# Experts ranked by token count on the chip, full ones in pairs of 64 slots, the emptiest four at a time in 32 slots, with weight loads addressed by registers

## Chip, core and metric

The kernel runs on 1 core of one Trainium2 chip. The metric is the device time of one execution in microseconds (us). A difference under about 0.2% (some 4.6 us) can't be told from no change.

## The reference, cut to the part that the change touches

The whole model is one hybrid layer (attention, retention, mixture of experts) and then two more layers with feed-forward blocks. The change touches only the routed experts of the first layer. There are 256 tokens of 1024 features and 64 experts; each token goes to 8 of them.

```python
def moe_ffn(h, router_w, router_bias, w1, w3, w2, sw1, sw3, sw2):
    scores = sigmoid(h @ router_w)                  # 256 x 64
    ...                                             # 4 of 8 groups, then top_e: 8 experts a token
    wts = wts / sum(wts) * ROUTED_SCALE
    for each expert e, for the tokens tok sent to e, with weight wt:
        xb = h[tok]
        yb = (silu(xb @ w1[e]) * (xb @ w3[e])) @ w2[e]     # 1024 -> 256 -> 1024, float32
        acc[tok] += yb * wt
    shared = (silu(h @ sw1) * (h @ sw3)) @ sw2
    return acc + shared
```

One expert's w1 and w3 are 2 MB together and its w2 is 1 MB, so the 64 experts have 192 MB of weights. How many tokens an expert gets is known only after the router has run. Evaluating the router on the inputs gives, for experts 0 to 7: 39, 36, 18, 42, 68, 25, 120 and 42 tokens. Four experts have more than 64 tokens (120, 77, 68, 67). The 64 counts add up to 2048. With experts 0 to 3 kept in front and the other 60 sorted, rank 4 has 120 tokens, rank 8 has 60, rank 39 has 25, rank 40 has 23 and rank 63 has 5.

## The kernel before

**Steps.** The routed experts are computed in 48 steps (`N_PAIRS`). A step fills the 128 partitions with 128 token slots. 32 of the steps are base steps: experts 2q and 2q+1 with 64 slots each. 16 are overflow steps: two blocks of 64 slots each for tokens that don't fit into an expert's first 64. Which expert an overflow block belongs to is decided on the chip. The order is written out by hand in `pair_order`: `"bbbb" + "obb" * 12 + "ob" * 4`. An overflow step runs on TensorE whether or not it has tokens.

**TensorE.** Each iteration i runs `gate_up(i)`, `hidden_turn(i - 1)` (two transposes), `gather_in(i + 1)` (eight transposes of the gathered token rows) and `down(i - 1)`. `gate_up` has 16 matmuls of a 128x64 stationary tile of tokens against 128x512 weights; the two experts of a step use different halves of the array's columns. `down` has 8 such matmuls. In the first 11 iterations `table(k)` runs too: small matmuls with one-hot matrices `OH` that turn the router's result into a token index and weight for each slot (`TAB`, then `IDX` and `WS` by VectorE's `post(k)`).

**Base weights.** SyncE (SP) issues 96 loads of 2 MB, two "up" and one "down" a base step, in the order of `NEED`, into five cells of the buffer `ring` (printed `ring<-in_exp_up`, `ring<-in_exp_down`). Load n waits until the load CELLS = 5 places before it has been used (`cell_read`) and until load n - 2 has landed (`cell_in`), so two are in flight.

**Gathers, overflow weights and scatters.** GpSimd (POOL) issues all indirect DMAs, in order. In turn i it issues the gather of the token rows for step i + 4 (L2041), then possibly the overflow weights (`overflow(k, "up")` and `overflow(k, "down")`, L2059, two DMAs each), then the scatter of step i - 1's result rows to `moe_rows` (L2068). Rows with an index outside the bounds are skipped, so an empty overflow block moves no weights; TensorE still waits for its semaphores `over_up` and `over_down`. The up weights of overflow step k are issued in the turn after the overflow step before it, and the down weights one turn later.

**Start.** SP loads five cells, then stores the normalised tokens to `h2_rows` (L744) as soon as their transposes are copied. The gathers wait for that store and for `posted`.

**After the steps.** SP fetches the first six weight tiles of the next feed-forward block and then reads `moe_rows` back in 8 loads.

Of the kernel before, what the change touches and what calls it, by code (L numbers as in the profile page):

```python
# [45 lines left out]
CAP = 64  # L46
N_BASE = N_EXP // 2
N_OVER = 16
N_PAIRS = N_BASE + N_OVER
N_BLOCKS = 2 * N_OVER  # L50
CELLS = 5
# [9 lines left out]
def pair_order():  # L61

    base, over = iter(range(N_BASE)), iter(range(N_BASE, N_PAIRS))
    kinds = "bbbb" + "obb" * 12 + "ob" * 4
    return [next(base) if k == "b" else next(over) for k in kinds]

def chunk_order():

    out = [0, 1]  # L70
    base, over = list(range(2, N_BASE // 2)), list(range(N_BASE // 2, N_PAIRS // 2))
    while base or over:
        out += over[:1] + base[:2]
        over, base = over[1:], base[2:]
    return out
# [3 lines left out]
PAIRS = pair_order()  # L79
CHUNKS = chunk_order()  # L80
# [13 lines left out]
def shape_constants():  # L94
# [49 lines left out]
    for h in range(4):  # L144
# [4 lines left out]
    own = np.stack([8 * p, 8 * (P + p), p + 1, P + p + 1], axis=1).astype(np.float32)  # L149
    rows = np.zeros((P, P), np.float32)  # L150
    rows[0:N_EXP] = p[0:N_EXP, None] * P + p[None, :] + 1
    moe = np.concatenate([wide(np.arange(1, CAP + 1)), own, wide(CAP * np.arange(N_BLOCKS)), wide(np.arange(N_BLOCKS)),
                          rows], axis=1).astype(np.float32)
    return {"k_before": before, "k_moe": moe, "k_heads": heads, "k_always": always, "k_dist": dist, "k_dirs": dirs, "k_chunk": chunk, "k_rot": rot}

def build(nc, A, out, h2_rows, moe_rows):
# [6 lines left out]
    with ctx:  # L164
# [34 lines left out]
        MC = sb("moe_const", [P, 260])  # L199
        IDX = sb("moe_index", [P, N_PAIRS, 2], I32)  # L200
        EIDX = sb("moe_expert_rows", [P, N_BLOCKS], I32)
        WS = sb("moe_slot_weight", [P, N_PAIRS])
# [120 lines left out]
        plan("sh_gate", 2, free=("hidden_ready", 1))  # L323
        plan("sh_up", 0, free=("hidden_ready", 1))
        plan("rank", 1)
        for n in range(4):
            plan(f"sh_y{n}", 3 + n, full=("units_down", 1))
        plan("ov_a", 0)
        plan("ov_b", 1)
        plan("ov_p", 7, free=("posted", 3))  # L330
        plan("moe_tab", 7, full=("table_full", len(CHUNKS)), free=("posted", len(CHUNKS)))
        for i in range(N_PAIRS):
            plan(f"mx{i}a", 0)
            plan(f"mx{i}b", 1)
            plan(f"mg{i}", 2 + i % 2)
            plan(f"mh{i}", 4)
            plan(f"my{i}a", 5)
            plan(f"my{i}b", 6)
# [3 lines left out]
        BASE_AT = [i for i in range(N_PAIRS) if PAIRS[i] < N_BASE]  # L342
        OVER_AT = [i for i in range(N_PAIRS) if PAIRS[i] >= N_BASE]
        NEED = []
        for i in range(N_PAIRS + 1):
            if i in BASE_AT:
                NEED += [(BASE_AT.index(i), "up_a"), (BASE_AT.index(i), "up_b")]
            if i - 1 in BASE_AT:
                NEED.append((BASE_AT.index(i - 1), "down"))
        CELL = {part: n for n, part in enumerate(NEED)}  # L350

        def cell(q, part):

            b = 7 + 2 * ((CELL[q, part] + 1) % CELLS)
            return BIG[:, b:b + 2, :]

        def cell_read(n):

            q, part = NEED[n]
            return uses[f"my{BASE_AT[q]}b" if part == "down" else f"mg{BASE_AT[q]}"].full  # L360

        def cell_in(n):

            return (f"cell_in{n % CELLS}", 16 * (n // CELLS + 1))
# [4 lines left out]

        posts_needed = {lp: CHUNKS.index(lp // 2) + 1 for lp in range(N_PAIRS)}  # L370
# [193 lines left out]
        OVER_DOWN = [BIG[:, 5 + e, :] for e in range(2)]  # L564
# [4 lines left out]
        P1 = MEAN[:, 0:4 * N_PAIRS].rearrange("p (l t b) -> p l t b", t=2, b=2)  # L569
        DW = K0[:, 256:256 + 12 * N_PAIRS].rearrange("p (l t b c) -> p l t b c", t=2, b=2, c=3)  # L570
# [3 lines left out]
        C_SLOT, C_ROW0, C_TOK, C_J64, C_J = MC[:, 0:64], MC[:, 64:66], MC[:, 66:68], MC[:, 68:100], MC[:, 100:132]  # L574
        C_EROW = MC[0:N_EXP, 132:260]
        OV_T = MIX[0:N_EXP, 4:7, :]
        OV_LO, OV_HI, OV_SEL, OV_TMP = (MIX[0:N_EXP, 7, a:a + n] for a, n in ((0, 1), (1, 1), (32, 32), (64, 32)))
        TAB = PS[:, 7, 0:6 * N_PAIRS].rearrange("p (l c) -> p l c", c=6)
        OVP = PS[:, 7, 288:480].rearrange("p (q t j) -> p q t j", q=3, t=2)
        OVE = PS[:, 7, 480:512]  # L580
# [66 lines left out]
        OV_N, OV_END, OV_BEG = (AXS[:, 6, 64 * a:64 * a + 64] for a in range(3))  # L647
        OV_OFF = AXS[:, 6, 192:256]
# [9 lines left out]
        CHKF = sb("chunk_row", [P, T])  # L658

# [26 lines left out]
        MASKED, RANKED, CHOSEN, ADDED = 1, 2, 3, 4  # L686
# [6 lines left out]
        def _(sp):  # L693
# [24 lines left out]
            def base(q, part, *free):  # L718

                n = CELL[q, part]  # L720
# [6 lines left out]
                if part == "down":  # L727
                    src = A["exp_down"][2 * q * P:(2 * q + 2) * P, :].rearrange("(e p) n -> p e n", e=2)
                else:
                    expert = 2 * q + (part == "up_b")  # L730
                    src = A["exp_up"][expert * P:(expert + 1) * P, :].rearrange("p (a n) -> p a n", a=2)
                sp.dma_start(cell(q, part), src).then_inc(S(cell_in(n)[0]), 16)
# [12 lines left out]
            for q, part in NEED[CELLS:]:  # L745
                base(q, part)
# [32 lines left out]
        def _(pe):  # L779
# [365 lines left out]
            for i in range(N_PAIRS):  # L1145
# [3 lines left out]
                if i + 1 < N_PAIRS:  # L1149
                    gather_in(i + 1)  # L1150
# [2036 lines left out]
```

## Time and profile before

| what | value |
|---|---|
| three runs | 2315.76, 2318.59, 2319.61 us; median 2318.59 us |
| profiled execution, its span | 2327.8 us |
| TensorE matmul busy | 2174.5 us, 93% |
| VectorE, ScalarE, GpSimd busy | 57%, 14%, 9% |
| HBM read / written | 634.49 / 27.26 MB |

The profile gives no time of its own for the profiled execution beside the span from its first to its last instruction; the span is 9.2 us above the median of the runs, which were executed without the profiler. Busy shares are averages over stages with different limits. Times in the rows below are counted from the start of the span. In lists by line, `x32` counts instructions; one float32 matmul of the program appears as two records.

### The profile page before, as it was taken

To read this page: it belongs to the slowest core of one execution; us is meant where nothing else is said; L and a number is where in the kernel's file an instruction comes from. 1 tells how busy PE (TensorE), PEld (TensorE's weight loads), DVE (VectorE), ACT (ScalarE), POOL (GpSimd) and SP (SyncE) were. 2 spreads that over 40 slices of the span, in tenths; PEclk is the share of its full clock that TensorE was granted. 3 is DMA by queue.
4 is the path that set the end of the run, shared out by engine and by line. 5 is a ranking of instruction groups with operands and counts; after the bars stand their busy time and mean duration, and the time that the engine had idled before them with its cause. 6 is when DMAs were issued, how large, how long until landed. Compare 5 with 4: busy or idle time off the path is not lost.

```text
span 2327.8 us, 32193 instructions
## 1 busy us (share of the span) xinstructions
PE 2174.5 (93%) x13280; PEld 1635.1 (70%) x13280; DVE 1329.9 (57%) x2488; ACT 322.2 (14%) x614; POOL 214.1 (9%) x264
## 2 busy tenths in 40 slices
PE   6999898989999989699999989999999998989997
PEld 3577753433333333499988868899989986579996
DVE  4567432321111111388875766798888876557774
ACT  2133100101111111100001341000000001430000
POOL 0000021223222222000000000000000000000000
PEclk9999899999999999899999999999999998999999
DMA  9865449989999986656666400566856663223441
GB/s 369 307 245 212 169 188 417 404 337 386 388 386 383 376 327 249 243 198 223 240 228 239 146 32 1 199 237 217 292 199 250 210 248 120 73 73 133 175 153 48
DMA packets 85969, 542.28 MB, mean 233 GB/s; under 512 B 24540, under 2 KB 24796, under 8 KB 33472
## 3 DMA queue, kind: packets, MB, share of 16 engines
q1 hardware_dynamic: 48448, 413.49, 46.5%
q0 software_dynamic: 36656, 124.83, 14.6%
q8 instruction: 106, 1.74, 0.3%
q10 hardware_dynamic: 720, 1.91, 0.2%
q14 instruction: 39, 0.32, 0.0%
HBM read 634.49 MB, written 27.26 MB: 284 GB/s over the span
## 4 chain that ended last, share of the span: by engine, by line
PE 84%; DVE 7%; DMA 7%; issue 1%; ACT 1%; POOL 0%; SPq 0%; DVEq 0%; POOLq 0%
PE ps L1190 30%; PE ps L1111 13%; PE ps L1140 6%; PE ps L979 3%; PE ps L1340 3%; PE ps L1245 3%; DMA ring<-in_exp_up,moe_expert_rows 3%; PE ps L1208 3%; PE ps L842 3%; PE ps L1090 2%; PE ps L868 1%; PE ps L1319 1%; DVE ring L2143 1%; PE ps L1586 1%; DVE x_streams L2143 1%
## 5 line engine op out<-in xcount | busy, mean ns | idle before, releaser
L1190 PEld LDWEIGHTS ps<-h,ring 128*128 128x128 f32 x4480 | 500.9, 192 | 0.2
L1190 PE MATMUL ps<-h,ring 128*128 128x128 f32 x4480 | 500.9, 275 | 0.0
L2143 DVE TENSOR_TENSOR ring<-ring 128x512 f32<-128x512 f32 (+5 forms) x411 | 349.3, 868 | 37.1 <-DMA ring<-moe_rows 22.6
L1111 PE MATMUL ps<-ring,h 128*64 128x512 f32 x1536 | 348.1, 607 | 22.9 <-DMA ring<-in_exp_up,moe_expert_rows 16.3
L1111 PEld LDWEIGHTS ps<-ring,h 128*64 128x64 f32 x1536 | 112.7, 140 | 242.7 <-issue 242.5
L2227 DVE SCALAR_TENSOR_TENSOR ring<-ring,ada_acc 128x1024 f32<-128x1024 f32 x152 | 179.6, 1222 | 42.0 <-DMA ring<-in_mod_w 30.3
L2537 DVE COPY hidden<-ps 128x256 f32<-128x256 f32 x48 | 20.4, 424 | 317.5 <-PE ps L1121 317.5
L1140 PE MATMUL ps<-ring,hidden 128*64 128x512 f32 x768 | 177.1, 603 | 7.2 <-DMA ring<-in_exp_down 4.4
L1190 PE MATMUL ps<-ring 128*128 128x128 f32 x1464 | 166.7, 275 | 0.0
L1190 PEld LDWEIGHTS ps<-ring 128*128 128x128 f32 x1464 | 165.4, 192 | 0.2
L2020 POOL DMA_DIRECT2D ring<-in_mod_w x72 | 38.7, 538 | 1000.9 <-DVE ring L2227 728.9
L1140 PEld LDWEIGHTS ps<-ring,hidden 128*64 128x64 f32 x768 | 52.2, 137 | 98.0 <-issue 98.0
L1811 ACT ACTIVATE silu_gate<-hidden 128x512 f32<-128x512 f32 x40 | 25.2, 631 | 492.0 <-DVE hidden L2143 492.0
L979 PE MATMUL ps<-h,ring 128*128 128x256 f32 x384 | 87.9, 390 | 3.2 <-DVE small L2362 1.1
L979 PEld LDWEIGHTS ps<-h,ring 128*128 128x128 f32 x384 | 74.5, 196 | 15.9 <-DVE small L2362 1.5
L1208 PE MATMUL ps<-h,ring 128*128 128x256 f32 x256 | 66.5, 428 | 19.5 <-DVE h L2148 19.5
L1340 PE MATMUL ps<-h,ring 128*128 128x256 f32 x384 | 84.1, 380 | 0.0
L1340 PEld LDWEIGHTS ps<-h,ring 128*128 128x128 f32 x384 | 72.7, 190 | 10.1 <-issue 0.3
L1779 ACT ACTIVATE silu_gate<-ps 128x256 f32<-128x256 f32 x48 | 18.4, 383 | 436.6 <-PE ps L1111 436.6
L2633 DVE COPY mean<-ps 128x256 f32<-128x256 f32 (+1 forms) x52 | 20.5, 393 | 101.5 <-PE ps L1190 101.4
L1208 PEld LDWEIGHTS ps<-h,ring 128*128 128x128 f32 x256 | 55.6, 219 | 30.5 <-issue 21.0
L1245 PE MATMUL ps<-ring 128*128 128x256 f32 x352 | 76.6, 379 | 0.0
(443 smaller groups left out, 2598.6 us busy)
## 6 DMA issues: line engine op xcount, KB each, us to landing
ring<-in_exp_up SPq DMA_DIRECT2D x64, 2048.0 KB, 10.8
ring<-in_mod_w POOLq DMA_DIRECT2D x72, 1024.0 KB, 6.8
ring<-in_exp_down SPq DMA_DIRECT2D x32, 2048.0 KB, 10.1
ring<-in_ffn_gate SPq DMA_DIRECT2D x44, 1024.0 KB, 4.8
ring<-in_ffn_up SPq DMA_DIRECT2D x44, 1024.0 KB, 6.2
ring<-in_ffn_down SPq DMA_DIRECT2D x32, 1024.0 KB, 4.9
ring<-in_ada_late POOLq DMA_DIRECT2D x16, 1024.0 KB, 5.2
ring<-in_hyb_in SPq DMA_DIRECT2D x16, 1024.0 KB, 6.0
```

The source lines that it names most:

```text
L842: last = mm(b[:, 0:(2 * T if wide else T)], w[:, kt, :], H[:, :, kt, :] if wide else H[:, 1, kt, :], start=kt == 0, stop=kt == KT - 1)
L979: last = mm(b[:, m * T:(m + 1) * T], w[:, kt, m * P:(m + 1) * P], MIX[:, kt, :], start=kt == 0 and m == 0, stop=kt == KT - 1 and m == 1)
L1090: last = nc.tensor.transpose(bs[k // 4][:, (k % 4) * P:(k % 4 + 1) * P], XG[i % LOOKAHEAD][:, k * P:(k + 1) * P], IDN)
L1111: last = mm(b[64 * e:64 * e + 64, :], xt[:, k // 2, k % 2, 64 * e:64 * e + 64], ws[e][:, k, :], start=k == 0, stop=k == KT - 1)
L1140: last = mm(bs[y][64 * e:64 * e + 64, :], ht[:, m, 64 * e:64 * e + 64], w[e][:, m, y * 512:(y + 1) * 512], start=m == 0, stop=m == 1)
L1190: ins = mm(dst, a[:, kt, :], b[:, kt, :], start=first and n < 2 and kt == 0, stop=last and n > 4 and kt == half - 1)
L1208: ins = mm(PS[:, u.bank, m * T:(m + 1) * T], w[:, kt, m * P:(m + 1) * P], U_IN[:, kt, :], start=kt == 0 and m == 0, stop=kt == KT - 1 and ...
L1245: ins = mm(y_of(6 + m), w[:, kt, m * P:(m + 1) * P], HIDA[:, k0 + kt, :], start=c == 0 and kt == 0 and m == 0, stop=z and kt == DOWN_KT[c] ...
L1340: last = mm(b[:, m * T:(m + 1) * T], w[:, kt, m * P:(m + 1) * P], U_IN[:, kt, :], start=kt == 0, stop=kt == KT - 1)
L2020: pool.dma_start(MR[:, slot, :], src).then_inc(S(f"mod_in{slot}"), 16)
L2143: return V.tensor_tensor(out_, a, b, op)
L2227: ins = V.scalar_tensor_tensor(out=w[:, h], in0=w[:, h], scalar=1.0, in1=row, op0=M, op1=M, accum_out=dst)
```

## The change

The experts are ranked on the chip by token count (counts are compared pairwise with VectorE, experts 0 to 3 are kept as ranks 0 to 3). 42 steps replace the 48, in a new fixed order. `pair` steps hold two experts of 64 slots. `second` steps hold the slots 64 to 127 of the pair just before (ranks 4 to 7), with the same weights. `quad` steps hold four experts of 32 slots (ranks 40 to 63). `over` steps, now 14, hold two overflow blocks. The numbers of `pair`, `quad`, `second` and `over` steps are 20, 6, 2 and 14. SP reads the expert's number from SBUF into a register for all loads but those of ranks 0 to 3. There are six cells. Overflow down weights now use the same buffer as the up weights.

```diff
-CAP = 64
-N_OVER = 16
-CELLS = 5
+CAP = 32
+FIXED = 4
+N_OVER = 14
+CELLS = 6
...
+def step_order():
+    kinds = "ff" + "dso" * 2 + "pqoppo" * 4 + "pqopo" + "qopop"
...
+def cap_of(rank):
+    if rank >= min(r for kind, r in STEPS if kind == "quad"):
+        return CAP
+    return 4 * CAP if ("second", rank - rank % 2) in STEPS else 2 * CAP
...
-        OVER_DOWN = [BIG[:, 5 + e, :] for e in range(2)]
+        OVER_DOWN = [BIG[:, 1 + 2 * e, :] for e in range(2)]
...
 # SP
+                if rank < FIXED:
+                    up = A["exp_up"][rank].rearrange("p (a n) -> p a n", a=2)
+                    downs = [A["exp_down"][rank + e] for e in range(2)]
                 else:
+                    sp.wait_ge(S("posted"), 1)
+                    who = [sp.value_load(EXI[0:1, rank + e:rank + e + 1], min_val=0, max_val=N_EXP - 1)
+                           for e in range(1 if part == "up" else 2)]
+                    up = A["exp_up"][bass.ds(who[0], 1)].rearrange("e p (a n) -> p (e a) n", a=2)
+                    downs = [A["exp_down"][bass.ds(w, 1)].rearrange("e p n -> p (e n)") for w in who]
+                if part == "up":
+                    sp.dma_start(cell(at, part, x), up).then_inc(landed, 16)
+                else:
+                    for e in range(2):
+                        sp.dma_start(cell(at, part, x)[:, e, :], downs[e]).then_inc(landed, 16)
...
             shared("shared_down", BIG[:, 4, :], (2,))
-            base(0, "down", released[23])
+            base(4, released[23])
+            base(5, released[21], released[22])
             for n in range(4):
                 wait(sp, uses[f"h2t{n}"].free)
             for tt in range(TT):
                 sp.dma_start(h2_rows[tt * P:(tt + 1) * P, :], H2T[:, tt, :]).then_inc(S("h2_stored"), 16)
...
-                last = uses[f"mg{o}"].full if slot < 3 else uses[f"my{o}b"].full if slot < 5 else cell_read(
-                    max(n for n in range(len(NEED)) if n % CELLS == 4))
+                last = uses[f"my{o}b"].full if slot < 3 else cell_read(
+                    max(n for n in range(len(NEED)) if n % CELLS == (5 if slot < 5 else 4)))
...
 # PE
+            def table(k):
+                pe.wait_ge(S("onehot"), k + 1)
+                for a in range(2):
+                    i = 2 * k + a
+                    dw = DW_F[:, i] if i < 2 else DW_S[:, i - 2]
+                    for tt in range(TT):
+                        for g in range(4):
+                            last = mm(TAB[32 * g:32 * g + 32, i, :], OH[k % 2][:, 8 * a + 4 * tt + g, :], dw[:, tt, g, :],
+                                      start=tt == 0, stop=tt == 1)
+                last.then_inc(S("table_full"), 1)
...
+                z = P // len(ws)
                 for k in range(KT):
-                    for e in range(2):
-                        last = mm(b[64 * e:64 * e + 64, :], xt[:, k // 2, k % 2, 64 * e:64 * e + 64], ws[e][:, k, :],
+                    for e, w in enumerate(ws):
+                        last = mm(b[z * e:z * e + z, :], xt[:, k // 2, k % 2, z * e:z * e + z], w[:, k, :],
                                   start=k == 0, stop=k == KT - 1)
...
 # POOL
             def overflow(k, kind):
-                if k == 0:
-                    pool.wait_ge(S("posted"), 3)
-                    if kind == "up":
-                        pool.wait_ge(S("units_down"), 1)
-                    else:
-                        for slot in (3, 4):
-                            wait(pool, released[18 + slot])
+                if kind == "down":
+                    wait(pool, uses[f"mg{OVER_AT[k]}"].full)
+                elif k == 0:
+                    pool.wait_ge(S("posted"), 2)
+                    pool.wait_ge(S("units_down"), 1)
                 else:
-                    o = OVER_AT[k - 1]
-                    wait(pool, uses[f"mg{o}" if kind == "up" else f"my{o}b"].full)
+                    wait(pool, uses[f"my{OVER_AT[k - 1]}b"].full)
...
-            for k in range(1, N_OVER):
-                up_turn[OVER_AT[k - 1] + 1] = k
-                down_turn[OVER_AT[k - 1] + 2] = k
+            up_turn = {OVER_AT[k - 1] + 2 if k else 0: k for k in range(N_OVER)}
...
-                if i in down_turn:
-                    overflow(down_turn[i], "down")
+                if i - 1 in OVER_AT:
+                    overflow(OVER_AT.index(i - 1), "down")
```

The tables of two steps now take 16 matmuls of a 128x32 stationary tile and 2 columns (4 of 128x128 and 6 columns before), and there are 21 of them (24 before). Ranking adds a chain of small operations on VectorE, TensorE and ScalarE between the router and the first gather.

**Where the order changes, first place: POOL near the end of the steps.** Each row is an indirect DMA: L2059 (L2161 in the changed kernel) loads overflow weights, L2041 (L2146) gathers rows for a later step, L2068 (L2170) scatters a result. Before:

```order
L2059 DMA ring<-in_exp_up,moe_expert_rows 128x4096 x2
L2068 DMA moe_rows<-ring,moe_index 2048x1024
L2041 DMA h<-h_rows,moe_index 128x1024
L2059 DMA ring<-in_exp_down,moe_expert_rows 128x2048 x2
L2068 DMA moe_rows<-ring,moe_index 2048x1024
```

The same engine in the middle of the changed kernel's steps, where overflow steps are three apart:

```order
L2146 DMA x_streams<-h_rows,moe_index 128x1024
L2161 DMA ring<-in_exp_down,moe_expert_rows 128x2048 x2
L2170 DMA moe_rows<-squares,moe_index 2048x1024
L2146 DMA x_streams<-h_rows,moe_index 128x1024
L2161 DMA ring<-in_exp_up,moe_expert_rows 128x4096 x2
L2170 DMA moe_rows<-ring,moe_index 2048x1024
```

The down load of an overflow step now comes first, one turn after that step's own gate_up, and the next overflow step's up load follows one turn later. Before, the up load came first and both were issued ahead of the step that uses them.

**Second place: SP between the prologue's loads and the first steps.** L744 (L803) is the store of the token rows; TENSOR_LOAD and ISA rows are the register reads. Before:

```order
L716 DMA ring<-in_shared_down 128x2048
L732 DMA ring<-in_exp_down 128x2x2048
L744 DMA h_rows<-squares 128x1024 x2
L732 DMA ring<-in_exp_up 128x4096 x2
L732 DMA ring<-in_exp_down 128x2x2048
```

And in the changed kernel:

```order
L764 DMA ring<-in_shared_down 128x2048
L790 DMA ring<-in_exp_down 128x2048 x2
L782 TENSOR_LOAD chunk_row
L782 ISA x2
L787 ISA
L787 DMA ring<-in_exp_up 128x4096
L803 DMA h_rows<-squares 128x1024 x2
```

The store of the token rows now stands behind a load that needs the ranking.

## Rows read from the trace of the kernel before

**Rows 1.** Windows of the step stage: engine busy times, granted clock, DMA share, GB/s.

```profile
316.00:499.00 183.00, 164.39 (x828) 74.16 (x828) 54.25 (x196) 16.75 (x32) 36.12 (x36) 0.93 0.91 372
499.00:841.00 342.00, 342.00 (x1690) 130.74 (x1689) 63.88 (x117) 46.12 (x88) 96.41 (x96) 1.00 0.98 383
841.00:944.00 103.00, 91.89 (x438) 34.46 (x436) 17.61 (x33) 12.23 (x23) 23.10 (x23) 0.95 0.64 244
```

**Rows 2.** Chain of waits, one step in the middle: start, duration, what.

```profile
504.19 6.87 PE ps L1111 x32
...
512.37 3.58 PE ps L1140 x16
515.95 6.87 PE ps L1111 x32
```

**Rows 3.** Chain of waits over the whole step stage, first, stalled and last pieces.

```profile
315.99 9.09 PE ps L1111 x32
...
326.11 1.68 PE ps L1059 x16
...
400.34 25.27 DMA ring<-in_exp_up,moe_expert_rows
...
850.77 14.96 DMA ring<-in_exp_up,moe_expert_rows
...
939.72 3.67 PE ps L1140 x16
...
953.01 19.81 DMA ring<-moe_rows
```

**Rows 4.** DMA by queue in 500 to 850 us: packets, MB, share.

```profile
q1 hardware_dynamic: 11132, 124.98, 89.9%
q0 software_dynamic: 13966, 8.89, 8.0%
```

**Rows 5.** Queue q0 alone, 300 to 325 us, then 325 to 500 us.

```profile
q0 software_dynamic: 576, 1.35, 18.1%
...
q0 software_dynamic: 5042, 17.62, 25.0%
```

**Rows 6.** Timeline at 857 us: a result copied, then POOL's issues.

```profile
857.04 0.69 DVE L2546 COPY ring<-ps 128x512 f32<-128x512 f32 x1 [2.90 <-PE ps L1140]
858.60 1.02 POOL L2068 DMA_INDIRECT moe_rows<-ring,moe_index  x1 [6.84 <-DVE ring L2546]
859.92 1.01 POOL L2041 DMA_INDIRECT h<-h_rows,moe_index  x1 [0.31 <-issue]
...
862.53 0.99 POOL L2059 DMA_INDIRECT ring<-in_exp_down,moe_expert_rows  x1 [0.30 <-issue]
```

**Rows 7.** L2059 (overflow loads), 500 to 850 us, then 840 to 855 us.

```profile
DMA to landing us min/median/max: 3.6/4.8/21.3
...
  PE ps L1111: 8.9, 1
...
DMA to landing us min/median/max: 4.7/9.8/15.0
```

**Rows 8.** Groups by line and shape: busy us, mean ns, idle before.

```profile
L842 PE MATMUL ps<-h,ring 128*128 128x512 f32 x96 | 42.2, 592 | 0.0
L1111 PE MATMUL ps<-ring,h 128*64 128x512 f32 x1536 | 348.1, 607 | 22.9 <-DMA ring<-in_exp_up,moe_expert_rows 16.3 <-DMA ring<-in_exp_up 5.6 <-issue 1.0
L1111 PEld LDWEIGHTS ps<-ring,h 128*64 128x64 f32 x1536 | 112.7, 140 | 242.7 <-issue 242.5
L813 PEld LDWEIGHTS ps<-ring,silu_c 128*2 128x2 f32 x128 | 5.7, 85 | 10.4 <-ACT hidden L1658 2.2 <-issue 0.8
```

**Rows 9.** Timeline of the start: SP's store, ScalarE, first gather.

```profile
285.02 0.83 SPq L744 DMA_DIRECT2D h_rows<-squares  x2
...
290.15 0.60 ACT L1760 ACTIVATE silu_gate<-ps 128x512 f32<-128x512 f32 x1 [3.91 <-PE ps L1031]
...
308.58 1.07 POOL L2041 DMA_INDIRECT x_streams<-h_rows,moe_index  x1 [75.82 <-DVE moe_index L2151]
```

More of the change, by code:

```diff
@@ L58, with step_blocks @@
 SILU_AT = {10: (0,), 11: (1,), 12: (2, 3), 13: (4, 5)}
[L61 to L75, printed above, removed]
+def step_order():
+    kinds = "ff" + "dso" * 2 + "pqoppo" * 4 + "pqopo" + "qopop"
+    pair, quad, over = 0, 2 * sum(kinds.count(k) for k in "fdp"), 0
+    steps = []
+    for k in kinds:
+        if k == "s":
+            steps.append(("second", pair - 2))
+        elif k == "o":
+            steps.append(("over", over))
+            over += 1
+        elif k == "q":
+            steps.append(("quad", quad))
+            quad += 4
+        else:
+            steps.append(("pair", pair))
+            pair += 2
+    return steps
+STEPS = step_order()
+N_STEPS = len(STEPS)
+N_TABLES = N_STEPS // 2
+SORTED = 4 * (N_STEPS - 2)
+def cap_of(rank):
+    if rank >= min(r for kind, r in STEPS if kind == "quad"):
+        return CAP
+    return 4 * CAP if ("second", rank - rank % 2) in STEPS else 2 * CAP
+def step_blocks(step):
+    kind, r = step
+    if kind == "quad":
+        return [(r + g, 0) for g in range(4)]
+    base = 2 * CAP if kind == "second" else 0
+    return [(r + g // 2, base + CAP * (g % 2)) for g in range(4)]
 HYB_COLS = [0, 256, 512, 768, 1536, 1792, 1024, 1280, 2120, 2376, 2632, 2888, 3144, 3400, 3664, 3920]
-PAIRS = pair_order()
-CHUNKS = chunk_order()
 PARAMS = {}
@@ L323, in build @@
         plan("sh_gate", 2, free=("hidden_ready", 1))
+        plan("rank", 1)
+        plan("ov_d", 7)
         plan("sh_up", 0, free=("hidden_ready", 1))
-        plan("rank", 1)
+        plan("ov_p", 1)
+        plan("ov_c", 7)
         for n in range(4):
             plan(f"sh_y{n}", 3 + n, full=("units_down", 1))
[L328 to L332, printed above, removed]
+        plan("sel_p", 0)
+        plan("sel_d", 2)
+        plan("sel_w", 1)
+        plan("moe_tab", 7, full=("table_full", N_TABLES), free=("posted", N_TABLES))
+        for i in range(N_STEPS):
             plan(f"mx{i}a", 0)
@@ L1085, in gather_in @@
+            for kt in range(4, KT):
+                last = shared_down(kt)
+            last.then_inc(S("units_down"), 1)
+            for name in ("sel_d", "sel_w"):
+                wait(pe, uses[name].free)
+            pe.wait_ge(S("posted"), 1)
+            table(1)
             def gather_in(i):
@@ L1102, in gate_up @@
                 else:
-                    parts = [(BASE_AT.index(i), "up_a"), (BASE_AT.index(i), "up_b")]
+                    at = i - 1 if kind == "second" else i
+                    parts = [(at, "up", x) for x in range(4 if kind == "quad" else 2)]
                     for part in parts:
@@ L1131, in down @@
                 else:
-                    part = (BASE_AT.index(i), "down")
-                    wait(pe, cell_in(CELL[part]))
-                    ws = [cell(*part)[:, e, :] for e in range(2)]
+                    at = i - 1 if kind == "second" else i
+                    parts = [(at, "down", x) for x in range(2 if kind == "quad" else 1)]
+                    for part in parts:
+                        wait(pe, cell_in(CELL[part]))
+                    ws = [cell(*part)[:, e, :] for part in parts for e in range(2)]
                 w = [x.rearrange("p (m n) -> p m n", m=2) for x in ws]
+                z = P // len(w)
                 ht = HID[:, i % 2, 1, :].rearrange("p (m n) -> p m n", m=2)
@@ L1144, in _ @@
             gather_in(0)
-            for i in range(N_PAIRS):
+            for i in range(N_STEPS):
                 gate_up(i)
```

393 lines of the change are left out of this document (215 added, 178 removed).

## The prediction

> **What bounds the kernel now.** I read three views in this order: the windows of the step stage, the chain of waits there, and the DMA queues. In the windows the reader is to see two resources that are full at once. From 499 to 841 us TensorE is busy all 342 us and the DMA share is 0.98 [rows 1]. The chain tells which of the two decides: it runs through TensorE alone, one step every 515.95 - 504.19 = 11.76 us, of which gate_up is 6.87 and down 3.58 [rows 2]. So this stretch is bound by TensorE, with DMA just behind it. The first stretch, 316 to 499 us, holds 12 steps. They should take 141.1 us, the tables of 11 steps add 11 x 1.7 to 2.0 = 19 to 22, and the first gate_up, at the lower clock after an idle time, 2.2 (9.09 against 6.87) [rows 2, 3]. That makes about 164; the rest, 19 us, is waiting, and the long piece in it is the 25.27 us load of overflow weights [rows 3]. These are real: queue q0 moved 17.62 MB from 325 to 500 us [rows 5], and four blocks of 3.15 MB are 12.6 of them. The number of blocks is four by the counts of the inputs (68, 120, 77, 67 tokens against 64 slots). That the trace ran these inputs shows in the first four gathers: 1.35 MB [rows 5] are 330 rows of 4096 bytes, and experts 0 to 7 are fetched by 330 of their tokens (39, 36, 18, 42, 64, 25, 64, 42). The last stretch has one stall: an overflow load that moves nothing took 15.0 us to land, and TensorE waited 8.9 us for it [rows 3, 7]. Steps end at 939.72 + 3.67 = 943.4 us.
>
> **What the change removes.** 48 steps become 42, which is 6 x 11.76 = 70.6 us of TensorE. After ranking, no expert has more tokens than its slots (rank 4 has 120 of 128, rank 8 has 60 of 64, rank 40 has 23 of 32), so the four real blocks and their 12.6 MB go. All 14 overflow steps are then empty. TensorE runs them all the same.
>
> **What DMA needs.** A load costs the queues 0.899 x 350 us / (124.98 / 2.097) = 5.28 us in the middle of the stage, and a gathered or scattered row 0.08 x 350 us / 2170 (8.89 MB / 4096 bytes) = 12.9 ns, skipped rows included [rows 4]. Where less else runs a load can be a little cheaper; I take 5.1. The 96 loads and 2 x 2048 rows are about 543 us, more than the 42 x 11.76 = 494 us of TensorE. So DMA may become the bound, and the 70.6 us can't all be won.
>
> **The start.** Half of the shared up-projection ends before ScalarE's silu at 290.15 [rows 9]. Ranking, four transposes and the other half follow, by the spacing of the old program to about 298; the first table and two small matmuls 2, VectorE's posting 2: posted at 302. Then SP reads a register, issues a 2 MB load and only then the store of the rows, which before was issued at 285.02 [rows 9]. The store lands behind that load: 5.1 + 4 + 1 makes 312. The gather takes 1.07 to issue [rows 9], some 4 to land, transposes and copy 3: first gate_up at 321, 5 us later than 315.99 [rows 3]. Bounds: -4 if the store overtakes the load, +9 if the ranking chain is slower.
>
> **Tables.** Each now has 32 records. The group nearest to a record with 32 stationary columns is the weight load of 2 columns, 5.7 us / 128 = 45 ns, below, and that of 64 columns, 112.7 / 1536 = 73 ns, above [rows 8]. I take 55: 1.76 us a table.
>
> **Quad steps.** 64 records in gate_up instead of 32. A record of 512 columns on the undivided array takes 42.2 / 96 = 440 ns, one on half the columns 348.1 / 1536 = 227 [rows 8]: two halves run side by side at 1.94 times. If four quarters do too, a record must start each 110 ns, more than the 73 ns that a 64-column weight load needs, so 6.87 us stays. I take that; the other bound is two at a time, 10.45 us more a quad step. The Trainium skill, TensorE: Matmul & The Clock Gate, in the table of tiled matmuls, gives 3.07 times for four tiles instead of 4. By it a quad step would be 3.2 us longer and six of them 19 us, mostly hidden by DMA; the rows speak for less loss, since two tiles lose only 3%. The sum keeps the rows' value.
>
> **A new wait.** An overflow step's down weights used to be issued ahead of the step, now only after the next gather. Let T be the end of the down-projection before. POOL's second DMA starts at T + 5.5 (857.04 to 862.53) [rows 6]; TensorE wants it after one gate_up and ten transposes, at T + 8.2. With a landing of 4.8, the median [rows 7], the stall is 2.1 us. Up weights start at T + 5.5 too, T now being the end of the last overflow step's down. If overflow steps are three apart TensorE wants them at T + 11.8: no stall. The last three (steps 36, 38, 40) are two apart: 5.5 + 4.8 = 10.3 us each, and 2.2 each for the lower clock after such an idle time. While TensorE stands, SP's loads behind its cells stand too.
>
> **The sum.** Steps 0 to 7: 8 x 11.76 + 2.2 + 16 tables x 1.76 = 124.5, ending at 445.5; TensorE bounds here, since eight steps need only 12 loads. Steps 8 to 31: TensorE needs 24 x 11.76 + 5.3 (tables) + 8 x 2.1 = 304; DMA needs 60 loads less 6 already in the cells, 54 x 5.1 = 275, and 2610 rows, 34, over a share of 0.98: 315. DMA decides, ending at 760.5. Steps 32 to 41: 117.6 + 4 x 2.1 + 3 x 12.5 = 163.5, ending at 924. One late landing as at 850 us: 9. Steps end at 933 instead of 943.4: -10. Behind them, three of the six feed-forward tiles are fetched only after the last step and come ahead of the read of `moe_rows` that takes 19.81 us [rows 3]: +3. Net -7 us: span 2321 instead of 2327.8. The span is 9.2 above the median of the runs, so the prediction is 2318.6 - 7 = 2312 us.
>
> SP's register reads (one for an up, two for a down load) aren't in the trace. I cost them at nothing, because load n waits for load n - 2 and load n - 1 still has its 5 us to go. If a read and issue take more than 5 us, each microsecond above costs up to 90 us in all; nothing suggests it.
>
> **Rivals.**
> - *Late landings (slower).* Landings between 500 and 850 us reach 21.3 us, and one of 15.0 stopped TensorE for 8.9 [rows 7]. Before, most such landings had some 12 us or more to spare; now 28 pairs stand on the path. One landing of 15 costs 12 us on a down and 9 on an up load. Beyond the one in my sum, the gain is gone with the second. One in five late makes 5 to 6: +35 to +45, about 2350. For it speaks that the DMA share will be near 1 in steps 8 to 31; against it that a late one is partly covered where TensorE waits for weights anyway, and that the median is 4.8. 
> - *Cheap extras (faster).* Tables at 45 ns a record (-6), store overtaking (-4), no late landing (-9), loads and steps interleaving well (-8): 2285.
> - *Quarters at half speed (slower).* 62.7 us of TensorE, of which some 20 to 25 hide under DMA: +40, 2350.
> - *The change does little*: what six steps save goes to loads and extras to within 4.6 us, 2318.
>
> **How the numbers follow.** My forecast -7 has a chance of 0.36 (its own range 2298 to 2326), cheap extras 0.21, late landings 0.27, quarters or register reads 0.10, nothing 0.06. The range over these is 2282 to 2356. Faster by over 0.2% (4.6 us): 0.24 of the forecast's case and 0.21 give 0.45. Within 0.2%: 0.08 and 0.05 give 0.13. Slower: 0.42.
>
> **What would show it.** First gate_up near 321 us; 42 steps; no q0 transfer of overflow weights; quad gate_ups of 6.9 us (13.7 if two at a time); waits of 2 us before each overflow down and of 10 us before the last three overflow gate_ups; loads the releaser in steps 8 to 31. Wrong if POOL's overflow landings, not loads, end most waits of TensorE in the middle stretch, or if quad steps are long.

## The result, and the profile after

The changed kernel takes **2386.79 us** (median of 4 runs, 2381.97 to 2393.83) against 2319.1 (2315.76 to 2322.53) for the kernel before, run beside it: ratio 1.0288, interval 1.0257 to 1.0319. That is 68 us slower, where I had forecast 2312 and a range up to 2356. The profiled execution has a span of 2380.2 us, 52 above the 2327.8 of before; the other 15 us come from how the two profiled spans stand to these medians (6.6 below, 8.7 above), which no row explains. Ratios and intervals leave out executions in which the chip was in its slower state, of which there was one, in run 9.

Line numbers after: L1183 `gather_in`, L1207 `gate_up`, L1240 `down`, L1129 `table`, L2161 `overflow`. First the windows of the changed kernel, cut as in [rows 1] (columns as there).

```profile
316.00:499.00 183.00, 162.50 (x1372) 68.17 (x1374) 48.65 (x142) 18.93 (x36) 41.81 (x41) 0.92 0.77 299
499.00:841.00 342.00, 285.70 (x1516) 107.72 (x1514) 50.49 (x92) 36.28 (x69) 76.91 (x77) 0.93 0.92 364
841.00:944.00 103.00, 60.02 (x308) 22.25 (x304) 9.95 (x19) 7.29 (x14) 14.11 (x15) 0.80 0.62 241
```

In the middle stretch TensorE was busy all 342 us before and is now for 285.7, and DMA fell from 0.98 to 0.92. **Neither resource is full any more**, so something is waiting that is neither TensorE's work nor the bytes. The waits of TensorE from 310 to 1010 us name it (total us, times, longest):

```profile
PE ps L1240 <- DMA ring<-in_exp_down,moe_expert_rows: 77.3, 13, 16.8
PE ps L1207 <- DMA ring<-in_exp_up,moe_expert_rows: 29.7, 3, 15.4
PE ps L1207 <- DMA ring<-in_exp_up: 22.2, 5, 6.0
PE ps L1183 <- DMA x_streams<-h_rows,moe_index: 7.0, 1, 7.0
```

107 us are waits for overflow transfers that move nothing. Before, waits for overflow transfers came to 17.5 us in four times; two of them, of 6.3 and 8.9 us, were for transfers that moved nothing. The 7.0 us of L1183 lie ahead of the first gate_up. The chain of waits in the middle shows the pattern, where [rows 2] had TensorE alone (start, duration, what):

```profile
563.53 17.40 DMA ring<-in_exp_down,moe_expert_rows
581.07 6.54 PE ps L1240 x16
...
616.65 7.94 DMA ring<-in_exp_down,moe_expert_rows
624.73 5.20 PE ps L1240 x16
...
717.82 3.65 PE ps L1240 x16
721.47 7.00 PE ps L1207 x64
```

One overflow step of each two lands after some 17 us, the other after 5 to 8. After ten of the 13 waits for downs the same 16 records of `down` take 5.2 to 6.6 us; after the other three (1.2, 2.4 and 2.9 us long) they take 3.65. The granted clock over the records at 581.07 is 0.51, the lower of its two levels:

```profile
581.00:587.00 6.00, 5.93 (x15) 1.91 (x16) 0.00 (x0) 0.60 (x1) 0.00 (x0) 0.51 0.99 406
```

Over the two later stretches it is 0.93 and 0.80 where it was 1.00 and 0.95.

Last, the start and the end of the chain:

```profile
302.29 10.46 DMA h_rows<-squares
...
320.73 8.74 PE ps L1207 x32
...
989.30 3.67 PE ps L1240 x16
...
994.55 8.35 DMA moe_rows<-ring,moe_index
...
1006.85 22.12 DMA ring<-moe_rows
```

The first gate_up starts at 320.73 and the steps end at 989.30 + 3.67 = 993.0, 49.6 later than before; from there to the end of the `moe_rows` reads (1028.97) it is 36.0 us, against 29.4 before. Together that is 56 us; the rest of the program took 3.8 us less than before, which makes the 52 of the spans.

The waits themselves, in the timeline of TensorE (start, duration, line, shape, count, idle time before and its releaser):

```profile
546.05 7.04 PE L1207 MATMUL ps<-ring,h 128*64 128x512 f32 x32
...
561.96 8.78 PE L1207 MATMUL ps<-ring,h 128*64 128x512 f32 x32 [3.99 <-DMA ring<-in_exp_up]
...
581.07 6.54 PE L1240 MATMUL ps<-ring,hidden 128*64 128x512 f32 x16 [9.02 <-DMA ring<-in_exp_down,moe_expert_rows]
...
595.72 3.65 PE L1240 MATMUL ps<-ring,hidden 128*64 128x512 f32 x16
...
862.92 5.57 PE L1240 MATMUL ps<-ring,hidden 128*64 128x512 f32 x16 [16.80 <-DMA ring<-in_exp_down,moe_expert_rows]
```

The 13 waits for downs are 7.2, 9.0, 8.7, 7.3 and 16.8 us behind the five landings of 17 to 23 us, together 49, and eight of 1.2 to 6.5, together 28. Each of the five is preceded by one of the five waits for a base up load (561.96 here): there the loads are behind already.

**Where TensorE's 672.3 us between the first gate_up and the end of the steps go.** 42 steps of 11.76 are 493.9. A step with the tables of two steps takes 12.61 (its gate_up starts at 344.06 and the next at 356.67), 0.85 more; nine of these and one with a single table are 8. The waits are 77.3 + 29.7 + 22.2 and 1.9 of other kinds, 131. The lower clock shows in the busy time of the groups. By line and shape outside quad steps (columns as in [rows 8]):

```profile
L1207 PE MATMUL ps<-ring,h 128*64 128x512 f32 x1152 | 268.7, 621 | 53.2 <-DMA ring<-in_exp_up,moe_expert_rows 29.7 <-DMA ring<-in_exp_up 22.2 <-issue 1.3
L1240 PE MATMUL ps<-ring,hidden 128*64 128x512 f32 x576 | 153.1, 680 | 78.9 <-DMA ring<-in_exp_down,moe_expert_rows 77.3 <-DVE hidden L2641 1.6
```

These are 36 `gate_up` of 32 records and 36 `down` of 16. At the full clock they take 7.04 and 3.65 us (546.05 and 595.72 above), so 36 x 7.04 = 253.4 and 36 x 3.65 = 131.4. `gate_up` is 15 us above that and `down` 22, together 37. All terms add up to 670 of the 672.3.

### The profile page after: what moved, and what is told of

Its sections match the earlier page's. It is cut to its first block, busy times and chain, and to the rows that moved or that the text cites. A ratio compares the mean times of both kernels' runs of the same rounds, so it can differ in the third digit from the quotient of the medians.

```text
span 2380.2 us, 33491 instructions
## 1 busy us (share of the span) xinstructions
PE 2111.9 (89%) x13714; PEld 1600.9 (67%) x13714; DVE 1308.8 (55%) x2409; ACT 313.6 (13%) x599; POOL 196.3 (8%) x244
## 3 DMA queue, kind: packets, MB, share of 16 engines
q0 software_dynamic: 33776, 112.24, 13.1%
## 4 chain that ended last, share of the span: by engine, by line
PE 78%; DMA 10%; DVE 7%; issue 2%; POOL 2%; ACT 1%; SPq 0%; POOLq 0%; DVEq 0%
PE ps L1290 30%; PE ps L1207 9%; PE ps L1240 7%; DMA ring<-in_exp_down,moe_expert_rows 6%; PE ps L1038 3%; PE ps L1440 3%; PE ps L1345 3%; PE ps L901 3%; PE ps L1308 3%; PE ps L927 1%; PE ps L1419 1%; PE ps L1183 1%; DVE ring L2241 1%; PE ps L1686 1%; DMA ring<-moe_rows 1%
## 5 line engine op out<-in xcount | busy, mean ns | idle before, releaser
L1207 PE MATMUL ps<-ring,h 128*64 128x512 f32 (+1 forms) x1536 | 311.1, 614 | 53.3 <-DMA ring<-in_exp_up,moe_expert_rows 29.7
L1207 PEld LDWEIGHTS ps<-ring,h 128*64 128x64 f32 (+1 forms) x1536 | 104.2, 135 | 248.8 <-issue 248.3
L1240 PE MATMUL ps<-ring,hidden 128*64 128x512 f32 (+1 forms) x768 | 174.9, 659 | 78.9 <-DMA ring<-in_exp_down,moe_expert_rows 77.3
L1240 PEld LDWEIGHTS ps<-ring,hidden 128*64 128x64 f32 (+1 forms) x768 | 51.7, 144 | 172.2 <-issue 172.2
L1440 PEld LDWEIGHTS ps<-h,ring 128*128 128x128 f32 x384 | 72.7, 190 | 10.1 <-issue 0.3
L2650 DVE COPY squares<-ps 128x512 f32<-128x512 f32 x20 | 13.8, 691 | 117.5 <-PE ps L1240 117.5
## 6 DMA issues: line engine op xcount, KB each, us to landing
ring<-in_exp_up SPq DMA_DIRECT2D x64, 2048.0 KB, 10.1
```

What stands on the lines that cost most here:

```text
L1207: last = mm(b[z * e:z * e + z, :], xt[:, k // 2, k % 2, z * e:z * e + z], w[:, k, :], start=k == 0, stop=k == KT - 1)
L1240: last = mm(bs[y][z * e:z * e + z, :], ht[:, m, z * e:z * e + z], w[e][:, m, y * 512:(y + 1) * 512], start=m == 0, stop=m == 1)
L1440: last = mm(b[:, m * T:(m + 1) * T], w[:, kt, m * P:(m + 1) * P], U_IN[:, kt, :], start=kt == 0, stop=kt == KT - 1)
```

## Experiments

All are timed against the kernel before. The first four undo or isolate one thing each.

**1. Down transfers issued one turn sooner.** POOL issues them in the overflow step's own turn, as soon as its gate_up is done and ahead of the scatter.

```diff
-                if i - 1 in OVER_AT:
-                    overflow(OVER_AT.index(i - 1), "down")
+                if i in OVER_AT:
+                    overflow(OVER_AT.index(i), "down")
```

> One edit to the changed kernel: POOL issues an overflow step's down weights in that step's own turn, ahead of the scatter of the step before, instead of one turn later behind that scatter and a gather. Theory 'late landings': TensorE's waits for overflow down weights (77.3 us in 13 waits in the changed kernel's profile) fall under 10 us, since the issue comes some 8 us earlier against 5.9 us of mean wait and the 17 us landings still cost a little; waits for base weights grow by 10 to 30 us because DMA catches up as the bound. Total 2317 to 2340 us instead of 2387. Rival 'DMA throughput is the bound': the waits only change their name to base weights and the total stays at 2377 or more.

Measured: **2347.89 us** (ratio 1.011, 1.0075 to 1.0146), 39 less than the changed kernel. Waits of TensorE:

```profile
PE ps L1207 <- DMA ring<-in_exp_up,moe_expert_rows: 72.0, 7, 16.2
...
PE ps L1240 <- DMA ring<-in_exp_down,moe_expert_rows: 1.6, 1, 1.6
```

The waits for downs go from 77.3 to 1.6 us. Those for overflow ups rise from 29.7 to 72.0, where I had expected base weights to take over (these stay at 23), and the time stands a little above the range that I gave.

**2. No overflow transfers.** The 14 overflow steps still run on TensorE, with whatever lies in their buffers; their DMAs and waits are left out.

> Leaves out all indirect loads of overflow weights and TensorE's waits for them; the 14 overflow steps still run, on whatever the buffer holds (their slots are empty). Theory 'late landings': this is the ceiling of what those loads cost, 77.3 + 29.7 us of waits less what the base weights then take over: 2285 to 2315 us. Rival 'DMA throughput': 2370 or more, with the waits on base weights.

Measured: **2290.42 us** (ratio 0.9868, 0.9845 to 0.9892). Of TensorE's waits for weights in the steps this one group stays:

```profile
PE ps L1206 <- DMA ring<-in_exp_up: 57.4, 10, 9.4
```

The change without its overflow transfers is 29 us faster than before. The 28 pairs of empty transfers cost 96 us.

**3. Smaller packets.** Each 2 MB up load as two of 1 MB, 8 KB a packet instead of 16.

```diff
-                    sp.dma_start(cell(at, part, x), up).then_inc(landed, 16)
+                    for h in range(2):
+                        sp.dma_start(cell(at, part, x)[:, h, :], up[:, h, :]).then_inc(landed, 16)
```

> Each 2 MB up load of the base weights is issued as two DMAs of 1 MB, whose packets are 8 KB instead of 16 KB; the bytes are the same. Theory 'skipped rows take turns with the packets of the weight loads': the landings of 17 to 23 us of the overflow down loads behind quad steps fall to about 10 us or less, and the total by 20 to 40 us (2347 to 2367). If the packets' size has nothing to do with it, the landings and the total stay (2380 to 2394).

Measured: **2388.62 us** (1.0289, 1.0263 to 1.0316): no change. The longest landing fell from 22.7 to 14.4 us and the waits for downs from 77.3 to 50.0, but the ups became late in seven places:

```profile
PE ps L1208 <- DMA ring<-in_exp_up,moe_expert_rows: 56.8, 7, 15.1
PE ps L1241 <- DMA ring<-in_exp_down,moe_expert_rows: 50.0, 13, 6.8
```

Packets of half the size go with a shorter longest landing, though not with the 10 us or less that I had expected; the sum of the two waits (107) did not move. What was won on one was lost on the other.

**4. No registers.** Loads take their expert from a fixed address (the weights are then not those of the ranks), so SP reads no register.

> All base weight loads take fixed addresses (the expert's number is the rank), so SP reads no registers; the experts' weights are then not those of the ranks, the work and bytes are the same. My prediction costs register reads at nothing: total within 6 us of the changed kernel's 2387. Rival 'register reads delay the loads': 10 us or more faster.

Measured: **2379.39 us** (1.0263, 1.0235 to 1.0291), 7 less, with an interval that overlaps that of the changed kernel. In the profiled executions the start is 3.6 us sooner, since no load waits for the ranking any more: the store goes out at 285.26 instead of 301.91, and the first gate_up starts at 317.10. But the steps end at 992.7, against 993.0 in the changed kernel: the waits for base ups fall from 22.2 to 14.5, those for overflow downs rise from 77.3 to 86.1. So the reads are not the slowdown, and this run can't tell their cost from nothing.

**5. Both transfers sooner.** As run 1, and the up transfers too one turn sooner (`OVER_AT[k - 1] + 1`).

> As the run with the early down load, and also the next overflow step's up weights one turn earlier, ahead of the scatter of the overflow step's result: issued about 4 us sooner after the buffer is free (T + 1.6 instead of T + 5.5). Theory 'late landings': waits for overflow up weights fall from 72 us to 30 us or less, and the total to 2300 to 2325 us, between the 2348 of the early down load and the 2290 of no overflow loads. Rival: the landing takes longer the earlier it is issued, since the same packets are in front; then 2335 or more.

Measured: **2322.25 us** (1.0015, 0.9996 to 1.0034): 65 less than the changed kernel, and no different from before. What is left of the waits:

```profile
PE ps L1207 <- DMA ring<-in_exp_up,moe_expert_rows: 37.4, 7, 15.8
PE ps L1207 <- DMA ring<-in_exp_up: 23.4, 6, 4.6
...
PE ps L1240 <- DMA ring<-in_exp_down,moe_expert_rows: 16.5, 5, 6.4
```

**6. And the row store ahead of the register load.** As run 5, with SP storing `h2_rows` before it asks for the sixth cell.

> As before, and SP stores the token rows ahead of the first register-addressed load. My prediction's start term (5 us later than before) says that this gives about 5 us or a bit more: first gate_up at 311 to 316 us instead of 320.7, total 4 to 9 us under that of both early issues.

Measured: **2317.93 us** (0.9984, 0.9969 to 0.9999), 4 less than run 5. The store goes out at 285.45 and the first gate_up starts at 317.28, against 320.10 in run 5: 3 us sooner, less than the 311 to 316 that I had expected. The load in front of the store costs some 4 us of the 10.46 that the store takes to land.

**7. Five cells, the overflow downs in a buffer of their own,** both overflow transfers issued where the kernel before issues them; ranking, 42 steps and registers stay, the store goes first.

```diff
-CELLS = 6
-OVER_DOWN = [BIG[:, 1 + 2 * e, :] for e in range(2)]
+CELLS = 5
+OVER_DOWN = [BIG[:, 5 + e, :] for e in range(2)]
```

> Undoes the buffer part of the change and keeps the ranking, the 42 steps and the register addresses: five cells, overflow down weights in a buffer of their own, both overflow loads issued at the turns of the kernel before, the token rows stored before any register-addressed load, the feed-forward tiles fetched as before. Theory 'late landings': TensorE's waits for overflow weights are under 20 us and the total comes near the run without overflow loads: 2285 to 2305 us, faster than the kernel before. Rival 'one cell less starves the quad steps', which need four cells at once: 2320 or more with the waits on base weights.

Measured: **2322.98 us** (1.0028, 1.0011 to 1.0045). The overflow waits are gone but for 5.6 us, and base weights take their place (the downs another 13.2 us):

```profile
PE ps L1206 <- DMA ring<-in_exp_up: 65.3, 11, 9.1
...
PE ps L1206 <- DMA ring<-in_exp_up,moe_expert_rows: 5.6, 2, 3.4
```

The rival in the expectation was right: with one cell less the loads run out. The sixth cell was paid for with the overflow downs' buffer. With the late issue that trade loses some 60 us against this run; with both transfers early (run 6) it gains 5.

**8. Quads one step earlier** in the pattern (`"qpoppo"` for `"pqoppo"`), since each late landing followed a quad step.

> Only the order of steps: each quad step stands before the pair step instead of after it, so that an overflow step never follows a quad step except in the last group. In the changed kernel the down weights of overflow steps right behind a quad land 17 to 23 us after issue, the others 5 to 8. Theory 'packets of up loads in front': a quad frees four cells at once and SP fills them with 16 KB packets just when POOL issues; with a pair between, the landings of 17 us fall to 5 to 8 us, total 2340 to 2370. If the delay belongs to every second overflow step whatever its neighbour, the total stays at 2380 or more.

Measured: **2396.76 us** (1.032, 1.0292 to 1.0348). Every second overflow step is still late, now with two pairs ahead of it where the quad was:

```profile
622.39 6.73 DMA ring<-in_exp_down,moe_expert_rows
...
671.04 14.01 DMA ring<-in_exp_down,moe_expert_rows
```

So the quad neighbour was not the reason, and my first theory here fell. What the late ones of the changed kernel share shows in SP's and POOL's timeline (start, duration until the last of the group, line, what):

```profile
550.63 12.31 SPq L787 DMA_DIRECT2D ring<-in_exp_up  x3
563.53 0.99 POOL L2161 DMA_INDIRECT ring<-in_exp_down,moe_expert_rows  x1 [0.30 <-issue]
...
604.71 7.51 SPq L787 DMA_DIRECT2D ring<-in_exp_up  x2
616.65 0.99 POOL L2161 DMA_INDIRECT ring<-in_exp_down,moe_expert_rows  x1 [0.30 <-issue]
619.39 4.19 SPq L790 DMA_DIRECT2D ring<-in_exp_down  x4
```

The transfer at 563.53 is issued within a microsecond of the third 2 MB load in a row and lands after 17.4 us; the one at 616.65 is issued 4.4 us after the last up load and lands after 7.9. In all five late cases SP asks for an up load between 1.7 us before and 1.8 us after the second transfer; before the six up to 802 us that land in 4 to 8 us the last load was asked for 4.8 to 5.1 us earlier (all counted from the start of the issue). In three of the five it is the third up load in a row, as here; the 22.7 us one (840.05) has an up load 1.7 us ahead and three more behind it. In run 8 three of the late ones stand right behind four loads of 1 MB instead, and one is issued 4 us after the last load, so how many loads it takes, and when, stays open. The DMA share is 1.00 around the first and 0.99 around the second, so the share does not tell them apart. Two things could: what the loads have already asked for, and the gather of rows just ahead in q0. Runs 9 and 10 are to part them.

**9. Downs ahead of the gather** of their turn, otherwise the changed kernel.

```diff
+                if i - 1 in OVER_AT:
+                    overflow(OVER_AT.index(i - 1), "down")
                 if i + LOOKAHEAD < N_STEPS:
                     gather(i + LOOKAHEAD)
```

> The changed kernel, with the two overflow down transfers of a step issued ahead of the row gather of the same turn of POOL, and not behind it; their wait is unchanged. Theory A (they land late because they stand in q0 behind a gather of rows that itself lands 8 to 15 us after its issue): the late landings of 17 to 23 us fall below 10 us, TensorE's wait for the overflow downs falls from 77 to under 30 us, total 2335 to 2355. Theory B (it is the full DMA engines alone, with up to 6 MB of loads asked for at once): landings stay at 14 us and more in five of 14 steps, the wait stays above 60 us, total 2375 to 2390.

Measured: **2394.07 us** (1.0284, 1.0219 to 1.0348). Landing of all overflow transfers, and waits:

```profile
DMA to landing us min/median/max: 2.1/6.4/20.3
```

```profile
PE ps L1207 <- DMA ring<-in_exp_up,moe_expert_rows: 72.6, 7, 15.2
PE ps L1240 <- DMA ring<-in_exp_down,moe_expert_rows: 40.4, 13, 9.6
```

The late downs still take 14.9, 15.2, 13.9, 10.4 and 18.4 us in the chain (mean 14.6, against 18.5 for the five of the changed kernel), so the gather in front is worth some 4 us of the lateness at most, not its bulk. Theory A's time is refuted, and theory B's wait (above 60) too: 40.4, with the ups 43 us worse instead.

**10. One load under way.** The changed kernel with `IN_FLIGHT = 1`.

> The changed kernel with a base load issued only when the load just before it has landed, in place of the one before that: at most one load of 2 MB is under way. Theory B (what is asked for at once delays the overflow transfers): the landings of 17 to 23 us fall to 10 or less and the wait for overflow downs from 77 to under 35 us; but a gap of about 2 us between loads is added, some 120 loads, so base waits rise by more than 50 us; total 2380 to 2480. Theory A (the gather in front): the landings stay above 14 us, since the gather is as slow as before, and the total is above 2450.

Measured: **2550.85 us** (1.0992, 1.0954 to 1.1031). The landings, and the waits:

```profile
DMA to landing us min/median/max: 2.1/6.9/10.1
```

```profile
PE ps L1207 <- DMA ring<-in_exp_up: 205.2, 18, 21.1
...
PE ps L1240 <- DMA ring<-in_exp_down,moe_expert_rows: 18.1, 4, 5.7
```

With the gather still in front and one load asked for at a time, no empty transfer lands later than 10.1 us. This fits theory B: what makes the 17 to 23 us is what the loads have asked for. One caution: the DMA share also fell, to 0.69 from 500 to 841 us, so depth and load were lowered together and this run does not part those two. The pacing itself cost far more than my top figure: the gap between loads is on the path everywhere.

**11. Both transfers sooner and ahead of the gather,** on top of run 6.

> The version with both overflow transfers one turn earlier and the row store first (2317.9 us), and both overflow transfers now ahead of the gather of their turn. Theory A (queue behind the gather): the waits for overflow ups and downs, 35.0 and 26.4 us there, fall by half or more, total 2285 to 2302. Theory B (full DMA engines): the two waits together stay above 50 us, total 2312 to 2322.

Measured: **2318.83 us** (0.9997, 0.9973 to 1.0022). Waits for overflow ups 36.7 and downs 16.0, 52.7 together (61.4 in run 6). Once the transfers are early, the gather hardly matters.

**12. Feed-forward tiles behind the `moe_rows` reads,** on top of run 6.

```diff
-                wait(sp, last)
-                fetch(first_units + slot)
+                if slot < 3:
+                    wait(sp, last)
+                    fetch(first_units + slot)
...
-            fetch_all(first_units + SLOTS, FFN_LOADS - SLOTS)
+            fetch_all(first_units + 3, FFN_LOADS - 3)
```

> The version with both overflow transfers one turn earlier and the row store first (2317.9 us), with the first feed-forward tiles of slots 3 to 5 asked for behind the reads of moe_rows and not ahead of them (slots 0 to 2 stay ahead). My theory (those 3 MB stand in front of the last scatter and of the 8 MB of moe_rows): the last scatter lands 4 to 5 us after its step, not 8.4, the moe_rows reads are in 2 to 6 us sooner, total 2306 to 2315, faster than before. Rival (the tiles are missed behind the reads, since the feed-forward starts 14 us after them): its first matmuls wait 4 us or more for tiles of slots 3 to 5, total 2315 to 2325.

Measured: **2311.79 us** (ratio 0.9962, 0.994 to 0.9983), the only complete version whose median is more than 0.2% below the kernel before. The end of its steps in the chain:

```profile
924.74 3.67 PE ps L1241 x16
...
929.96 3.99 DMA moe_rows<-ring,moe_index
...
937.61 19.78 DMA ring<-moe_rows
```

The last scatter lands in 3.99 us instead of 8.35 and the reads in 19.78 instead of 22.12. From the last `down` to the end of the reads it is 29.0 us, against 36.0 in the changed kernel, and no matmul behind the reads waits for a tile. The kernel before was not tried with this order, so the 6 us against run 6 may be open to it too.

## Why the prediction was wrong, point by point

**The step that failed** is "A new wait": "With a landing of 4.8, the median [rows 7], the stall is 2.1 us." The mechanism, its place and its issue time were right: in the middle a second down transfer is issued at 563.53, 5.5 us after the down-projection's end at 554.40 + 3.61 = 558.0. The size was not. I took the median of landings that nobody had waited for; with the new order five of 14 meet loads that are just being asked for and take 17 to 23 us. And I let most of these stalls hide under a stretch bound by DMA, where they did not hide: they came on top.

Against the 933 - 321 = 612 us of the sum, the 672.3 measured are made up so:

| term | in the sum | measured |
|---|---|---|
| 42 steps of 11.76 | 493.9 | 493.9 |
| waits for overflow downs | 8.4 on the path (21 more hidden or left out) | 77.3 |
| waits for overflow ups, a late one included | 3 x 10.3 + 9 = 39.9 | 29.7 |
| base loads slower than TensorE | 315 - 24 x 11.76 - 5.3 = 27.5 | 22.2 |
| lower clock | 2.2 + 3 x 2.2 = 8.8 | 37 |
| tables | 28.2 + 5.3 = 33.5 | 8 |
| other waits | 0 | 1.9 |

The downs are 69 us too low and the clock 28, the tables 25 too high. Runs 1, 5 and 2 show the first on the chip: issuing the downs sooner takes 39 us, the ups too 26 more, and with none to wait for 96 are gone. That the loads asked for at that time set the landing is supported by run 10, with its caution, and by run 3, but not shown apart from the load on DMA.

**The rival of late landings** was the right one. It had five or six late ones at 9 to 12 us each; five came, and cost 49 us. Its 2350 fell short of 2387 because it kept 2.1 us, mostly hidden, for the others, which took 28, and no lower clock behind the downs, which took 22 more. The Trainium skill, DMA: Bandwidth & Descriptors, section SWDGE vs HWDGE vs iDMA (an engine takes turns between the two kinds of queue) fits run 3, where halving the packet took the longest landing from 22.7 to 14.4 us; that the waits did not shrink there it does not explain.

**The start**: 321 predicted, 320.73 measured. The store issued at 302, behind the load, and landed at 312.8, 312 in my sum: right. Run 6 shows 4 us for the load in front, of my 5.1.

**Tables**: mis-sized in the harmless direction. I took 55 ns a record and 1.76 us a table. The 32 records of a table, on four column strips in turn, start within 0.28 us, 9 ns each, and all tables together cost 25 us less than in my sum:

```profile
330.42 0.43 PE L1129 MATMUL ps<-always,expert_weight 128*32 128x2 f32 x32
330.70 0.44 PE L1129 MATMUL ps<-always,broadcast_params 128*32 128x2 f32 x32
```

The weight loads that I priced it by are 105 to 114 ns each by their own duration, but they overlap; spacing, not the nearest group's busy share, was the number.

**Quad steps**: 6.87 kept, 7.00 measured for 64 records. Four quarters side by side lose 2%, so the rival at half speed is out, and so is the 3.2 us a step that I worked out from the Trainium skill, TensorE: Matmul & The Clock Gate, section Measured speedup vs the span model. Its 3.07 times is for four row tiles of 32 rows; the quad steps use four column tiles.

**Overflow weights gone**: right; q0 moved 112.24 MB in the whole execution, 124.83 before.

**DMA as the bound in the middle**: right for run 2, which has no overflow transfers (its waits there are all for base ups), but the floor lay higher than mine. My sum without the overflow terms (8.4, 3 x 12.5 and 9) ends the steps at 878; run 2 ends them at 908.9. Its waits for base ups by stretch, 445 to 760 and 760 to 910 us:

```profile
PE ps L1206 <- DMA ring<-in_exp_up: 44.3, 7, 9.4
...
PE ps L1206 <- DMA ring<-in_exp_up: 13.1, 3, 6.0
```

I had 27.5 in the first and nothing in the second, where I let TensorE decide alone.

**SP's register reads**: costed at nothing, and run 4 can't tell them from nothing.

**The tail**: +3 predicted, +6.6 measured. I saw the three tiles in front of the `moe_rows` reads but not that they stand in front of the last scatter too (8.35 us, 4.40 before). Run 12 gives it back.

**A reading of the kernel before**: of the 19 us of waiting in the first stretch I put the long piece down to the real overflow load of 25.27 us. TensorE waited 1.2 us for that one. It waited 6.3 for the next, which was issued at 444.95 and landed after 31.33 us:

```profile
444.95 31.33 DMA ring<-in_exp_up,moe_expert_rows
...
476.42 9.09 PE L1111 MATMUL ps<-ring,h 128*64 128x512 f32 x32 [6.26 <-DMA ring<-in_exp_up,moe_expert_rows]
...
q0 software_dynamic: 1300, 1.00, 9.7%
```

From 445 to 476 us q0 moved 1.00 MB in all (the last line: packets, MB, share), gathers included, and one real overflow up load is 2.1 MB, so this one moved nothing. The trace before thus had two empty transfers that landed late and stopped TensorE, and I priced one.

**Where the six steps' 70.6 us went**: by run 2 the change leaves 29 of them at most when the overflow transfers cost nothing, since base loads fill DMA (share 0.96 from 499 to 841 us there); the overflow transfers, issued later than before because their downs now share the ups' buffer, then take 96.

## What to carry to other kernels

Price a new wait on a DMA by the upper landings under the load that will be there, not by the median of landings nobody waited for, and count the lower clock behind each stop. A transfer that moves nothing still has to be issued early: here such transfers landed after 2 to 23 us, one in the kernel before after 31. When a buffer is freed by aliasing two others, look first at which issue the aliasing moves to the far side of a wait.

## What the runs showed of the hardware

- Indirect DMAs whose rows are all skipped landed after 2.1 to 22.7 us in the changed kernel, and one before after 31.3. It was 17 to 23 five times in the changed kernel, each time with a 2 MB load asked for between 1.7 us before and 1.8 us after it, some 4 less without a gather in front of it, at most 14.4 with 8 KB packets, at most 10.1 with one load under way.
- Matmul records with 32 stationary columns and 2 moving columns, on four column strips in turn, started every 9 ns.
- Four 32-column tiles run side by side at 64 records in 7.00 us, against 32 of two tiles in 6.87.
- After ten of the changed kernel's 13 waits for overflow downs, 16 records of 3.65 us took 5.2 to 6.6, and after its three waits for overflow ups, 32 records of 7.04 us took 8.5 to 9.2. The granted clock was 0.51 from 581 to 587 us and 0.80 from 841 to 944.
